# Squares of each norm moved into the product before it, one activation table for logarithm and exponential, x loaded by chunks

## The reference, cut to what matters

```python
def rms_norm(x, g):
    y = xf * lax.rsqrt(jnp.mean(xf * xf, axis=-1, keepdims=True) + EPS)
    return (y * g).astype(x.dtype)
...
        h = rms_norm(x, norm1_g[l])
        proj = h @ w_in[l]
        ...
        x = x + jnp.concatenate([ym, ya], axis=-1) @ w_out[l]
        h2 = rms_norm(x, norm2_g[l])
        x = x + peer(h2, ...)
...
        h = modulate(rmsnorm(x, g_attn[i]), sh1, sc1)
        hc = modulate(rmsnorm(ctx, g_attn[i]), sh1c, sc1c)
        ...
        x = x + gt1 * (o @ w_out)
        h = modulate(rmsnorm(x, g_ffn[i]), sh2, sc2)
        x = x + gt2 * conv_ffn(h, ...)
```

## Time and profile before

| what | value |
|---|---|
| median of 3 runs | 4164.61 us (4163.69 to 4170.68) |
| the profiled execution's own time | 4165.35 us |
| its span, first to last instruction | 4163.6 us |
| PE busy | 3747.8 us, 90% |
| DVE, ACT, POOL busy | 2646.9, 1400.6, 1353.3 us |
| mean granted clock of TensorE | 0.94 |

### The profile page before, as it was taken

How to read it: one execution, slowest core, us unless ns; L and a number is a source line. 1 busy time by engine, 2 the same in 40 slices (tenths; PEclk the granted TensorE clock), 3 DMA queues, 4 the chain that set the end, 5 groups by cost and what they waited for, 6 DMA issues and landing times. The chain is left out here.

```text
span 4163.6 us, 56639 instructions
## 1 busy us (share of the span) xinstructions
PE 3747.8 (90%) x19146; PEld 3030.6 (73%) x19146; DVE 2646.9 (64%) x5270; ACT 1400.6 (34%) x1945; POOL 1353.3 (33%) x578
## 2 busy tenths in 40 slices
PE   7857889999999989999989988889998987788989
PEld 5643677778888778888877756568887865566867
DVE  6554778887777689999988446565454032745440
ACT  3204323335555322223232147622222122454331
POOL 3002333443333344444433126412222220343433
PEclk9957899999999999999999989989999988899999
DMA  5202444444554666566644340221111111012222
GB/s 196 63 13 81 151 141 140 146 140 144 188 178 159 224 222 194 190 197 190 197 147 152 96 79 1 77 96 61 65 55 55 56 41 33 6 41 91 95 77 89
DMA packets 242793, 475.43 MB, mean 114 GB/s; under 512 B 47195, under 2 KB 127067, under 8 KB 237692
## 3 DMA queue, kind: packets, MB, share of 16 engines
q1 hardware_dynamic: 223516, 435.11, 32.2%
q10 hardware_dynamic: 19152, 38.81, 2.5%
HBM read 397.82 MB, written 71.83 MB: 113 GB/s over the span
## 5 line engine op out<-in xcount | busy, mean ns | idle before, releaser
L265 POOL TENSOR_TENSOR w_low<-w_raw,w_high 128x1024 fp32r<-128x1024 f32 (+1 forms) x204 | 535.7, 2627 | 1164.8 <-ACT w_high L229 1164.8
L179 PE MATMUL psum<-h_high,w_high 128*128 128x512 f32 (+1 forms) x1696 | 624.4, 368 | 83.6 <-DVE h_low L473 55.1
L180 PE MATMUL psum<-h_low,w_high 128*128 128x512 f32 (+1 forms) x1696 | 618.5, 365 | 0.0
L181 PE MATMUL psum<-h_high,w_low 128*128 128x512 f32 (+1 forms) x1696 | 613.4, 362 | 0.0
L229 ACT ACTIVATE w_high<-w_raw 128x1024 fp32r<-128x1024 f32 (+1 forms) x204 | 226.4, 1111 | 942.0 <-PE psum L181 899.6
L1405 POOL TENSOR_TENSOR pick_u_low<-pick_u_raw,pick_u_high 128x1024 fp32r<-128x1024 f32 x128 | 312.2, 2439 | 569.1 <-ACT pick_u_high L1459 569.1
L1649 POOL TENSOR_TENSOR v_low<-v_raw,v_high 128x1024 fp32r<-128x1024 f32 x128 | 308.1, 2408 | 400.1 <-ACT v_high L1639 400.1
L179 PEld LDWEIGHTS psum<-h_high,w_high 128*128 128x128 f32 x1696 | 322.8, 190 | 154.7 <-issue 71.4
L179 PE MATMUL psum<-a_high,v_high 128*128 128x512 f32 x1024 | 399.2, 390 | 16.8 <-DVE a_low L1681 16.8
L179 PE MATMUL psum<-h_high,pick_u_high 128*128 128x512 f32 x1024 | 412.1, 402 | 0.9 <-POOL pick_u_low L1405 0.9
L180 PE MATMUL psum<-h_low,pick_u_high 128*128 128x512 f32 x1024 | 403.1, 394 | 0.0
(11 more groups left out here) (368 smaller groups left out, 7053.9 us busy)
## 6 DMA issues: line engine op xcount, KB each, us to landing
pick_u_raw<-in_expert_uT SPq DMA_DIRECT2D x128, 512.0 KB, 3.5
v_raw<-in_expert_v SPq DMA_DIRECT2D x128, 512.0 KB, 3.9
mod_w<-in_w_mod SPq DMA_DIRECT2D x88, 512.0 KB, 3.7
w_raw<-in_ffn_up SPq DMA_DIRECT2D x88, 512.0 KB, 3.4
gelu_dram<-pick_gelu ACTq DMA_DIRECT2D x128, 256.0 KB, 2.0
gates_dram<-gate_plane SPq DMA_DIRECT2D x32, 1024.0 KB, 7.5
g<-gates_dram SPq DMA_DIRECT2D x64, 512.0 KB, 5.1
p<-gelu_dram SPq DMA_DIRECT2D x128, 256.0 KB, 5.0
```

Source lines behind the costliest of these rows:

```text
L179: nc.tensor.matmul(bank, w_high, x_high, start=first, stop=False)
L180: nc.tensor.matmul(bank, w_high, x_low, start=False, stop=False)
L181: return nc.tensor.matmul(bank, w_low, x_high, start=False, stop=last)
L265: nc.gpsimd.tensor_tensor(w_low[r % 2][:, :, :], raw[r % n_raw][:, :, :], w_high[r % 2][:, :, :].bitcast(F32), ALU.subtract).then_inc(k.w_ ...
```

## The change

Five edits. (1) `stage_load` is gone. The first product loads x in 8 chunks on SP's queue ahead of the weights, constants and parameters on ACT's queue ahead of the condition, and the context on ACT's queue after the second weight block is rounded; squares of the first norm wait chunk by chunk. (2) For the other five norms the squares, their sum and the product with ones are done in the stage before (class `Squares`): ACT squares chunk c after the epilogue that finishes it, POOL adds chunks 1 to 6 up, and PE makes two calls with the ones at the end, one on the sum of seven chunks and one on chunk 7. In these products ACT's and POOL's loops are written out. (3) The context's part for norm 3, which PEER does not alter, is squared and summed at the head of `stage_values`; PE's loop there waits until DVE has copied the result. (4) ACT is told at the head of each norm to load the table set that has both Ln and Exp. (5) `low` follows `scaled` by one chunk and not by two.

```diff
-def stage_load(k, t): ...
+class Loads:
+    def x(self, sp):
+        for c in range(KD):
+            sp.dma_start(self.k.xT[:, c, 0:SEQ], self.t["xT"][:, c, :]).then_inc(self.x_in[c].sem, 16)
+    def tables(self, act):
+        act.dma_start(self.k.consts[:, :], self.t["consts"]).then_inc(self.tables_in, 16)
+        act.dma_start(self.k.params[:, :], self.t["params"]).then_inc(self.tables_in, 16)
+    def context(self, act):
+        act.dma_start(self.k.xT[:, :, SEQ:TOK], self.t["ctxT"]).then_inc(self.context_in, 16)
+class Squares:
+    def __init__(self, k, pieces):
+        ...
+        n = 2 if self.width <= SEQ else 1
+        ...
+    def square(self, act, c):
+        if c > len(self.sq):
+            act.wait_ge(self.added.sem, self.added.at(c - len(self.sq)))
+        self.nc.scalar.activation(self.slot(c)[:, :], self.k.xT[:, c, 0:self.width], ACT.Square).then_inc(self.squared.sem, 1)
+    def add(self, pool, c):
+        pool.wait_ge(self.squared.sem, self.squared.at(c + 1))
+        if c > 1:
+            pool.wait_ge(self.added.sem, self.added.at(c - 1))
+        self.nc.gpsimd.tensor_tensor(self.acc[:, :], self.acc[:, :], self.slot(c)[:, :], ALU.add).then_inc(self.added.sem, 1)
+    def total(self, pe):
+        pe.wait_ge(self.added.sem, self.added.at(KD - 2))
+        for i, (t0, n) in enumerate(self.pieces):
+            self.nc.tensor.matmul(self.k.psum[:, i, 0:n], self.k.const("ones"), self.acc[:, t0:t0 + n], start=True, stop=False)
+        pe.wait_ge(self.squared.sem, self.squared.at(KD))
+        for i, (t0, n) in enumerate(self.pieces):
+            mm = self.nc.tensor.matmul(self.k.psum[:, i, 0:n], self.k.const("ones"), self.slot(KD - 1)[:, t0:t0 + n], start=False, stop=True)
+        mm.then_inc(self.sum_ready.sem, 1)
 def product(...):
     def _(act):
+        if norm and norm.loads:
+            norm.loads.tables(act)
         if side:
             side.load_cond(act)
...
             norm.squares(act)
             round_weights(0, 0)
             round_weights(0, 1)
+            if norm.loads:
+                norm.loads.context(act)
             norm.scalar(act)
...
+        if sums:
+            for it in range(passes):
+                for r in range(RING):
+                    if it * RING + r + 2 < passes * RING:
+                        round_weights(it, r + 2)
+                    if r % parts == parts - 1:
+                        c = it * per + r // parts
+                        act.wait_ge(k.bank_read.sem, k.bank_read.at((per + c + 1) * n_pieces))
+                        sums.square(act, c)
+            return
     def _(pool):
+        if sums:
+            for it in range(passes):
+                for r in range(RING):
+                    weights_low(it, r)
+                    c = it * per + r // parts - 2
+                    if r % parts == parts - 1 and c > 0:
+                        sums.add(pool, c)
+            sums.add(pool, n_chunks - 2)
+            return
     def _(pe):
...
+        if sums:
+            sums.total(pe)
 class Norm:
     def squares(self, act):
-        for c in range(KD): ...
+        self.nc.scalar.preload_act_table_set("natural_log_exp_and_others")
+        if self.loads:
+            for c in range(KD):
+                act.wait_ge(self.loads.x_in[c].sem, self.loads.x_in[c].at(16))
+                ...
-        for c in range(KD + 2):
+        for c in range(KD + 1):
             if c < KD:
                 scaled(c)
-            if c >= 2:
-                low(c - 2)
+            if c >= 1:
+                low(c - 1)
 def stage_values(k, t, f):
         def _(act):
+            nc.scalar.activation(context_sq[:, :, :], k.xT[:, :, SEQ:TOK], ACT.Square).then_inc(context_squared, 1)
...
+            for c in range(KD):
+                act.wait_ge(x_added, times * 32 + (c + 1))
+                sums.square(act, c)
         def _(pool):
...
+            for c in range(1, KD - 1):
+                sums.add(pool, c)
         def _(pe):
             pe.sem_inc(out_summed, 2 * KD)
+            pe.wait_ge(context_squared, 1)
+            for c in range(KD):
+                mm = nc.tensor.matmul(k.psum[:, KD - 1, 0:CTX], k.const("ones"), context_sq[:, c, :], start=(c == 0), stop=(c == KD - 1))
+            mm.then_inc(context_summed, 1)
+            pe.wait_ge(context_taken, 1)
             with pe.Fori(0, times) as it:
...
+            sums.total(pe)
         def _(dve):
             prepare(0, 0)
             prepare(0, 1)
+            dve.wait_ge(context_summed, 1)
+            nc.vector.tensor_scalar(k.v_context[:, :], k.psum[:, KD - 1, 0:CTX], 1.0 / D, EPS, ALU.mult, ALU.add).then_inc(context_taken, 1)
```

More of the change, by code:

```diff
@@ L159, with __init__ @@
 PIECES = ((0, SEQ), (SEQ, CTX))
[L162 to L172, removed]
+class Loads:
+    def __init__(self, k, t):
+        self.k, self.t = k, t
+        self.x_in = [k.shared(f"chunk_in{c}") for c in range(KD)]
+        self.tables_in, self.context_in = k.sem("tables_in"), k.sem("context_in")
+    def x(self, sp):
[6 more added lines that the diff above has]
+        act.dma_start(self.k.xT[:, :, SEQ:TOK], self.t["ctxT"]).then_inc(self.context_in, 16)
@@ L209, in _ @@
     def _(sp):
+        if norm and norm.loads:
+            norm.loads.x(sp)
         with sp.Fori(0, passes) as it:
@@ L217, in _ @@
                     side.load(sp, it, r)
+        if norm and norm.loads:
+            sp.wait_ge(norm.loads.context_in, 16)
     @block.scalar
     def _(act):
+        if norm and norm.loads:
+            norm.loads.tables(act)
         if side:
@@ L401, with __init__ @@
 class Norm:
-    def __init__(self, k, pieces, gain, shift=None, first=None):
+    def __init__(self, k, pieces, gain, shift=None, first=None, loads=None, v_context=None):
         self.k, self.nc, self.pieces, self.gain, self.shift, self.first = k, k.nc, pieces, gain, shift, first
+        self.loads, self.v_context = loads, v_context
         k.names += 1
@@ L438, in tensor @@
         k = self.k
+        if not self.loads:
+            return
+        pe.wait_ge(self.loads.tables_in, 32)
         for c in range(0, KD, 2):
@@ L1265, in first_block @@
         high, low = k.place("mix_high", BIG, KD, SEQ, dtype=FR), k.place("mix_low", BIG + KD * SEQ, KD, SEQ, dtype=FR)
-        product(k, block, t["w_out"], KD, KD, LATENT, high, low, BIG + 2 * KD * SEQ, add_to_x(k, lambda c, i: 1.0, LATENT), full=f.mixT,
+        product(k, block, t["w_out"], KD, KD, LATENT, high, low, BIG + 2 * KD * SEQ, add_to_x(k, lambda c, i: 1.0, LATENT), full=f.mixT, sums=Squares(k, LATENT),
                 side=Modulation(k, t, ((2 * KD, 1, 2),), 40000, 34816))
@@ L1733, in gains @@
             k.dve(dve, k.nc.vector.scalar_tensor_tensor(k.gain[:, i, :], k.modT[:, j:j + KD, i], 1.0, k.par(name, layer * KD, KD), ALU.add, ALU.mult))
-    return Norm(k, pieces, lambda i, c: k.gain[:, i, c:c + 1], lambda i, c: mod_col(k, layer, first, c, i), gains)
+    return Norm(k, pieces, lambda i, c: k.gain[:, i, c:c + 1], lambda i, c: mod_col(k, layer, first, c, i), gains, v_context=v_context)
 class NaTable:
@@ L1817, in na_layer @@
         high, low = split_of_q(k, "na", layer)
-        product(k, block, t["na_o"], KD, KD, both, high, low, FREE, add_to_x(k, lambda c, i: mod_col(k, layer, 2, c, i), both), full=b.q,
+        product(k, block, t["na_o"], KD, KD, both, high, low, FREE, add_to_x(k, lambda c, i: mod_col(k, layer, 2, c, i), both), full=b.q, sums=Squares(k, both),
                 side=Modulation(k, t, ((MODS + 4 * KD, 2, 1), (MODS + 4 * KD + 1, 2, 1)), BIG + 2 * KD * TOK, BIG + 2 * KD * TOK + 2 * D, 43008))
@@ L1884, in swa_layer @@
         high, low = split_of_q(k, "swa", layer)
-        product(k, block, t["swa_o"], KD, KD, LATENT, high, low, FREE, add_to_x(k, lambda c, i: mod_col(k, layer, 2, c, i), LATENT), full=b.q)
+        product(k, block, t["swa_o"], KD, KD, LATENT, high, low, FREE, add_to_x(k, lambda c, i: mod_col(k, layer, 2, c, i), LATENT), full=b.q,
+                sums=Squares(k, LATENT))
 def conv_ffn(k, t, layer, pieces):
@@ L1944, in build @@
     k = Core(nc)
-    stage_load(k, t)
     first_block(k, t)
```

63 lines of the change are left out of this document (46 added, 17 removed).

## The result

| | before | after |
|---|---|---|
| median of 22 runs each | 4163.60 us (4160.70 to 4170.68) | 4172.16 us (4168.70 to 4174.53) |
| ratio, 95% interval | | 1.0019 [1.0012, 1.0026] |
| profiled execution | 4165.35 us | 4169.04 us |

The changed kernel is 8.6 us slower; I had 5.3 us faster, and 4172.16 lies outside the range. The profiled execution after is one of its fastest, so the two traces differ by only 3.7 us: I read stages from the traces, and the size of the whole from medians.

A forecast was written before the change was run, and what follows sets the result against it. PE, busy 90%, could gain only at waits for DVE: 55.1 us at five norms, 16.8 at `stage_values`. Terms 7.6 - 7.7 - 2.6 + 0.0 + 2.9 + 3.1 + 0.7 + 1.3 gave 5.3 us faster, 4159.3; range 4150 to 4170.

The forecast's parts named there:

- Rival (b): POOL's addition in `w_out` and the tail of `stage_values` costs 2.4 us: 13.8 us more, 4173; chance 0.08.
- `low` one chunk behind: In the norms, PE starts 0.6 to 1 us earlier but gains nothing: zero, with 0.3 per norm either side.
- The port in `w_out`: DVE's products wait for POOL's additions, period about 5.9 us; last addition to x 3.3 us late, bounds 0 to 5.
- The tail of `stage_values`: At that stage's end, before norm 3, POOL's additions at 1.2 us each set a tail 2.6 us late.
- the wait for the context's copy: At the head of `stage_values`, PE waits for DVE's copy behind `prepare(0, 1)`: 7.7 us late, bounds 6 to 8.5.
- the first block: In norm 1, earlier weights put Ln at 20.6 for 26.90, one table load saved: 7.6 us gained, bounds 5.5 to 9.
- the tails of `na_o` and `ffn_down`: At the ends of these 768-column stages, a last square and two ones calls delay the next stage 2.5 us each.
- the norm over heads: In layer 1, it finds the table set still loaded and loses one load from its chain: 1.3 us gained.
- the other five norms: Norms 2 to 6 start their products sooner: 2.6, 2.6, 5.4, 5.6 and 2.6 us gained ahead of the tails.
- rival (d): In the norms the table set doesn't stay, so thirteen loads of 1.3 us come back: 4176; chance 0.04.
- The table term: Every norm loses two table loads of 1.3 us, 2.6 us, through one set for Ln and Exp.

The follow-up runs named there:

- the two other pairs: `low` one against two chunks behind: loads and table set alone, 4155.55 against 4150.53; squares of norms 4 and 5 moved, unread PE calls added, 4151.65 against 4147.83.
- e1: The changed kernel with DVE's copy of the context's mean moved ahead of `prepare(0, 0)`: 4164.27 us, ratio 0.9997.
- the extra calls: Four or five unread PE calls per norm before the first product, added to chunked loads, one table set, low two behind, squares of norms 4 and 5 moved: 4147.83 us.

## Why the prediction was wrong

The forecast and the median are 12.9 us apart, and 13.9 if each is taken against its own "before". Three steps account for 13.5 of it: 7.4 (a median; 6.0 by the traces), 3.6 (with the tail of `w_out`) and 2.5. Rival (b) had 4173, but only by luck is that near: its addition of 2.4 us was not found, and over half of the miss is edit 5, which it left at nothing.

*`low` one chunk behind: "Zero, with 0.3 per norm to each side".* It cost 7.4 us in the changed kernel, 5.0 and 3.8 in the two other pairs. I counted DVE's steps, saw that PE starts sooner (by 0.8 us in norm 4) and had the last `low` up to 0.3 us later; it is 0.3 later in norm 2 and 0.5 in norm 4. I knew that PE starts at its lower clock level, and took from it that the order is worth nothing. The step that failed is that I asked when the first product starts and not when PE's last gap ends: the clock rises behind that gap, 29.7 to 31.3 us into norm 5 with low two behind and 32.6 to 33.3 with low one, at half a microsecond each. I also left out that in norm 2 the stage is DVE's to the end, where the meeting of DVE with POOL shifts (2.3 of the 6.0 us). For norm 4 the order's share stays open.

*The port in `w_out`: 3.3 us.* It cost 6.7. I put POOL's addition at 1.2 us by a slope between 1024 and 1408 columns, and that was nearly right: it takes 1.26 to 1.30 us in `stage_values` and `swa_o`. In `w_out` it takes 1.51 to 1.65 and once 2.27, and the rest is waiting. What I had wrong is who waits: I summed the port's load to a period of 5.9 us and let only DVE's products wait. POOL's subtraction waits too (3.38 for 2.40), then `modT` behind it (2.02 for 0.23), and while DVE adds to x, 0.69 us, POOL has nothing to do, since its addition needs that x squared; 5.9 and 0.7 are about the 6.59 measured, though this sum is an estimate from the rows and no run takes it apart. ACT and PE come behind. The cost is of the kind that rival (b) had, but its reason, a dear addition, is not what the rows show. The Trainium skill's "SBUF — State Buffer", section "SBUF: two separate sides", says that whichever of the two starts first holds the pair of ports that DVE and POOL share for its whole instruction, and the other fully blocks. The rows of `w_out` after agree, in both directions; that rule spoke against my sum, and I had used one half of it.

*The tail of `stage_values`: 2.6 us.* It is 5.1. Six additions take 8.43 us with the hand-overs between them, not 7.2; ACT's last two squares wait for POOL's slots; and the two calls with the ones find PE at its lower level after a wait, 2.08 and 1.71 us with 0.85 for an instruction where I had 0.43.

What held: the wait for the context's copy (7.7 forecast; 8.2 at the first product, 7.9 by e1), the first block (7.6; 8.1), the tails of `na_o` and `ffn_down` (2.5 each; 2.3 and 2.9), the norm over heads (1.3; 0.9), and with low two behind the other five norms within 0.5 us. That the table set stays, rival (d), is seen in norm 1; its loads took 1.28 us each and no gap beside them. The table term was too high only for a kernel that I did not forecast, with the squares left in place. Two of the terms that held did so in part by luck. In norm 1, 5.67 MB at the rate that the loading of x shows, 339 GB/s, would give 20.0 us and not the 19.2 that I took. The rounding was released at 17.65, so that Ln came 8.0 us sooner where I had 6.3 and PE's first product 9.1; but the clock's rise came only 6.6 us sooner (38.6 and 32.0), and the stage gained 8.1. In norm 4 too Ln came 5.0 us sooner where I had 4.1.

## What to carry to other kernels

Move work ahead only for the branch that ends last in that stage: by the stages of the traces, squares in the stage before paid in norms 4 and 5, where the sum was last, and lost in norms 2 and 3, where their cover was a busy port or no cover at all. When DVE and POOL share a port and both are in a loop, don't add up the port's load alone: follow one round of the loop, let each of them wait for the other, and count the time in which neither can use it. Here additions of 512 columns, 1.29 us alone, took the period from 5.44 to 6.59 us, and additions of 32 columns left it. PE that followed DVE with gaps of 0.47 us was at its lower clock in these norms, so judge an order of work by when the last gap ends and not by when the first product starts.

## What the hardware showed that I had not expected

An addition of 32 columns on POOL takes 1.24 us where it starts 1.1 us ahead of the end of DVE's product, and 0.50 where it starts 0.4 us ahead of it; both end 0.1 us behind the product. So nearly all of a short POOL instruction in such a loop can be waiting. Timeline of the second case, in the version with thin additions:

```profile
455.22 1.22 DVE L468 SCALAR_TENSOR_TENSOR mod_products<-mod_w,mod_cond 128x1024 bf16<-128x1024 f32 x1
456.04 0.50 POOL L220 TENSOR_TENSOR squares_sum<-squares_sum,squares 128x32 f32<-128x32 f32 x1 [3.34 <-ACT squares L214]
```

The clock that the extra calls had raised in norm 5 was down again before DVE's last `h_low`, while PE worked with gaps, and in norm 6, where it stayed up, it brought nothing.
